# Projection of q, k, v in chunks of 512 columns instead of 384, with attention steps due at the ends of unbroken slots

## What is computed

```
hn   = rms_norm(x)                                  # 1024 x 1024
proj = hn @ w_in + b_in
q, k, v of 3 groups x 4 heads x 128 channels        # 12 units of 3 x 128 columns
q, k = rope(rms_norm(q)), rope(rms_norm(k))
out, lse = windowed attention of each group          # dilation 1, 4, 16
att  = softmax over the groups' lse, weighted sum of the outs
y_att = att * silu(z_att);  y_rnn = RG-LRU branch
x = x + (gate0 * (y_rnn @ w_o_rnn) + gate1 * (y_att @ w_o_att)) @ w_out
x = x + sigmoid(rms_norm(x) @ w_ple_gate + b) * (p @ w_ple)
```

## Time and profile before

| | us |
|---|---|
| median of 3 runs | 1463.46 |
| lowest and highest | 1462.47, 1465.11 |
| span of the profiled execution | 1463.9 |

### The profile page before, as it was taken

The page is one execution under the profiler, slowest core; times in us unless marked ns, Lnnn a source line. Parts: engine busy times, 40 slices in busy tenths (PEclk is TensorE's granted clock), DMA queues, the critical chain, the costliest instruction groups (busy, mean ns, idle before and its releaser), DMA issues.

```text
span 1463.9 us, 20230 instructions
## 1 busy us (share of the span) xinstructions
PE 1444.7 (99%) x6830; PEld 1282.4 (88%) x6830; DVE 833.2 (57%) x1698; ACT 455.9 (31%) x1162; POOL 507.7 (35%) x496
## 2 busy tenths in 40 slices
PE   8899999999999999999999999999999999999998
PEld 6688888999999999999999998888888888888887
DVE  5999998847764555654555666117822346325323
ACT  6345454533332332332322336520110001223100
POOL 6755544333321320330320433336543333243120
PEclk9999999999999999999999999999999999999999
DMA  6222312241211111110110113246628843321111
GB/s 230 80 79 80 106 61 96 86 128 50 64 42 37 49 44 49 49 53 26 49 52 32 58 58 116 87 144 244 222 79 327 305 151 108 122 72 37 51 51 43
DMA packets 67354, 139.76 MB, mean 95 GB/s; under 512 B 8672, under 2 KB 22976, under 8 KB 67264
## 3 DMA queue, kind: packets, MB, share of 16 engines
q10 hardware_dynamic: 29968, 75.89, 14.3%
q1 hardware_dynamic: 37296, 62.69, 13.6%
HBM read 109.04 MB, written 29.51 MB: 95 GB/s over the span
## 4 chain that ended last, share of the span: by engine, by line
PE 96%; DVE 2%; issue 0%; ACT 0%; DMA 0%; SPq 0%; DVEq 0%; ACTq 0%
PE bank L1068 30%; PE bank L1073 29%; PE bank L1072 29%; PE bank L1206 2%; PE bank L1186 2%; PE bank L1175 1%; PE bank L1195 1%; DVE xc L804 1%; PE bank L1293 0%; DMA x_nat<-in_x 0%; PE bank L1104 0%; DVE qkn L888 0%; DVE xc_lo L814 0%; DVE qks L902 0%; DVE qkr L901 0%
## 5 line engine op out<-in xcount | busy, mean ns | idle before, releaser
L398 POOL TENSOR_TENSOR w_lo<-raw,w_hi 128x512 fp32r<-128x512 f32 (+1 forms) x245 | 319.7, 1305 | 890.6 <-PE bank L1073 816.4
L1068 PE MATMUL bank<-w_hi,hn_hi 128*128 128x384 f32 x768 | 301.1, 392 | 0.0
L1073 PE MATMUL bank<-w_hi,hn_lo 128*128 128x384 f32 x768 | 290.7, 378 | 0.0
L1072 PE MATMUL bank<-w_lo,hn_hi 128*128 128x384 f32 x768 | 290.2, 378 | 0.0
L1068 PE MATMUL bank<-hn_hi,w_hi 128*128 128x512 f32 x640 | 251.6, 393 | 1.2 <-DVE hn_lo L749 1.2
L1073 PE MATMUL bank<-hn_hi,w_lo 128*128 128x512 f32 x640 | 249.7, 390 | 0.0
L1072 PE MATMUL bank<-hn_lo,w_hi 128*128 128x512 f32 x640 | 249.6, 390 | 0.0
L1072 PEld LDWEIGHTS bank<-w_lo,hn_hi 128*128 128x128 f32 x768 | 219.3, 286 | 0.0
L1073 PEld LDWEIGHTS bank<-w_hi,hn_lo 128*128 128x128 f32 x768 | 219.3, 286 | 0.0
L1068 PEld LDWEIGHTS bank<-w_hi,hn_hi 128*128 128x128 f32 x768 | 217.8, 284 | 0.1
L402 POOL TENSOR_SCALAR w_hi<-raw 128x512 fp32r<-128x512 f32 (+1 forms) x245 | 195.0, 796 | 9.1 <-DMA raw<-in_w_rnn_s 9.1
(11 more groups left out here) (176 smaller groups left out, 2097.7 us busy)
## 6 DMA issues: line engine op xcount, KB each, us to landing
raw<-in_w_tail_s SPq DMA_DIRECT2D x104, 256.0 KB, 2.6
raw<-in_w_qkv_s SPq DMA_DIRECT2D x96, 192.0 KB, 2.3
g_in<-gate_dram ACTq DMA_DIRECT2D x48, 256.0 KB, 3.0
raw<-in_w_rnn_s SPq DMA_DIRECT2D x45, 256.0 KB, 2.6
gate_dram<-g_out ACTq DMA_DIRECT2D x32, 256.0 KB, 2.0
o_dram<-o_buf ACTq DMA_DIRECT2D x12, 512.0 KB, 2.6
o_in<-o_dram ACTq DMA_DIRECT2D x12, 512.0 KB, 4.1
wt_in<-mw_dram ACTq DMA_DIRECT2D x12, 512.0 KB, 4.7
```

What stands on the lines that cost most here:

```text
L398: nc.gpsimd.tensor_tensor(w_lo[:, p % RING, 0:width], raw[:, p % RAW, 0:width], w_hi[:, p % RING, 0:width].bitcast(F32), ALU.subtract).the ...
L1068: ins = T.matmul(out, lhs[0], rhs[0], start=first, stop=False)
L1072: T.matmul(out, lhs[0], rhs[1], start=False, stop=False)
L1073: return T.matmul(out, lhs[1], rhs[0], start=False, stop=last)
```

## The change

- The 4608 columns of q, k, v are cut in 9 chunks of 512 (three to a group) instead of 12 units of 384: 72 slots of 24 matmuls with 512 columns. A chunk holds 4 parts of 128 columns, which belong to two heads; `part_of` and `parts_in` translate. Each weight piece is loaded by two DMAs from the unchanged array.
- The attention steps are no longer bound to slots. There are 101 steps (96 tiles and the last lag); step A stands behind the slot in which 90 + 6A blocks of contraction are done (`STEPS_AT`), so behind a slot come one or two steps, and they run on into the gate slots. The lags between parts are now counted in steps: 0 for the rotation, 1, 3, 4, 5. All three engines follow one list, `MAIN_ORDER`: slot, then its steps. DVE's work of a slot is `take_qkv`, ACT's the squares.
- In the gate slots ACT serves the gate first and then the steps. Two gates more stand before the first z, so two fewer after the last.
- qkv has three chunk buffers; to make room the ring has 12 pieces while q, k, v, gates and z run, outputs are written out in halves, and the rotation tables are held for one group at a time and loaded in halves.
- SP's and POOL's loops are written out instead of looped.

```diff
-LAG_T, LAG_QK, LAG_ET, LAG_PV = 9, 11, 12, 13
+LAG_T, LAG_QK, LAG_ET, LAG_PV = 1, 3, 4, 5
+STEPS = TILES + LAG_PV
+FIRST_STEP, STEP_BLOCKS = 90, 6
+STEPS_AT = [[A for A in range(STEPS) if -(-(FIRST_STEP + STEP_BLOCKS * A) // KD) == slot + 1]
+            for slot in range(SLOTS_Q + len(Z_MAIN))]
+
+
+def main_order():
+
+    order = []
+    for slot in range(SLOTS_Q + len(Z_MAIN)):
+        order.append(("slot", slot))
+        order += [("step", A) for A in STEPS_AT[slot]]
+    return order
...
+def ring_slot(p):
+
+    if p < FIRST_QKV:
+        return p % RING
+    if p < FIRST_O:
+        return (p - FIRST_QKV) % RING_Q
+    return (p - FIRST_O) % RING
...
-Z_MAIN = [(kind, t, h) for kind, t in [("gate", t) for t in range(10)]
-          + [("z", 0), ("gate", 10), ("z", 1), ("gate", 11), ("z", 2), ("gate", 12), ("z", 3)]
-          + [("gate", t) for t in range(13, 16)] for h in range(2)]
...
+Z_MAIN = [(kind, t, h) for kind, t in [("gate", t) for t in range(11)]
+          + [("z", 0), ("gate", 11), ("z", 1), ("gate", 12), ("z", 2), ("gate", 13), ("z", 3)]
+          + [("gate", t) for t in range(14, 16)] for h in range(2)]
...
+            for p in range(RAW, PIECES):
+                sp.wait_ge(w_ready, p + 1 - RAW)
...
+                    for u, col, width, dst in chunk_sources(c):
+                        sp.dma_start(raw[:, p % RAW, dst:dst + width], a["w_qkv_s"][u * KD + k, :, col:col + width]
+                                     ).then_inc(raw_in[p % RAW], 16)
...
+            for what, G in MAIN_ORDER:
+                if what == "step":
+                    attention(G)
+                    continue
+                if G < SLOTS_Q:
+                    if G >= 3:
+                        take_qkv(G)
+                    continue
...
-            for G in range(SLOTS_A):
-                u, s = divmod(G, NT)
-                grp = u // HEADS
+            for G in range(SLOTS_Q):
+                c, s = divmod(G, NT)
                 n = N_A + G
                 bank_free(n)
-                hi, lo = positions(grp, s, hn_hi), positions(grp, s, hn_lo)
+                hi, lo = positions(c // 3, s, hn_hi), positions(c // 3, s, hn_lo)
                 for k in range(KD):
-                    p = FIRST_QKV + KD * u + k
+                    p = FIRST_QKV + KD * c + k
                     need(p)
-                    ins = passes(bank[n % 4][:, 0:QKV], (hi(k), lo(k)),
-                                 (w_hi[:, p % RING, 0:QKV], w_lo[:, p % RING, 0:QKV]), k == 0, k == KD - 1)
+                    ins = passes(bank[n % 4][:], (hi(k), lo(k)), part(p), k == 0, k == KD - 1)
...
-                attention(G)
-
+                for A in STEPS_AT[G]:
+                    attention(A)
```

More of the change, by code:

```diff
@@ L59 @@
 RING = 16
+RING_Q = 12
 FIRST_QKV = PIECES_RNN
@@ L107, in has_prev, with part_of, parts_in, chunk_sources @@
     return (g == 0 and tile > 0) or (g == 1 and tile % 2 == 1)
+def part_of(u, x):
+    g, h = divmod(u, HEADS)
+    c, b = divmod(3 * h + x, CHUNK)
+    return 3 * g + c, b
+def parts_in(c):
+    g, r = divmod(c, 3)
+    return [(HEADS * g + (CHUNK * r + b) // 3, (CHUNK * r + b) % 3, b) for b in range(CHUNK)]
+def chunk_sources(c):
+    g, r = divmod(c, 3)
+    u, col = HEADS * g + CHUNK * r // 3, CHUNK * r % 3 * HD
+    width = 3 * HD - col
+    return (u, col, width, 0), (u + 1, 0, HALF - width, width)
+def raw_count(p):
+    loads = [2 if FIRST_QKV <= o < FIRST_TAIL else 1 for o in range(p % RAW, p + 1, RAW)]
+    return 16 * sum(loads)
+def units_after(c):
+    g, r = divmod(c, 3)
+    return [HEADS * g + h for h in ((0,), (1, 2), (3,))[r]]
+def std_count(u):
+    return 3 * (u // HEADS) + (0, 1, 1, 2)[u % HEADS] + 1
 def group_rows(stat, w, g, hd):
-    first = (w * SLOTS_A + (g * HEADS + hd) * NT) * P
+    first = (w * TILES + (g * HEADS + hd) * NT) * P
     classes = CLASSES[g]
@@ L373, in _ @@
                 sp.dma_start(dst[:], a[src]).then_inc(chan_in, 16)
[L374 to L387, removed]
+            for c in range(2):
+                sp.dma_start(bias_qkv[:, c], chunk_bias(c)).then_inc(bq_in[c], 16)
+            for p in range(RAW, PIECES):
+                sp.wait_ge(w_ready, p + 1 - RAW)
+                if p < FIRST_QKV:
+                    load(p % RAW, a["w_rnn_s"][p])
+                elif p < FIRST_TAIL:
+                    c, k = divmod(p - FIRST_QKV, KD)
+                    for u, col, width, dst in chunk_sources(c):
+                        sp.dma_start(raw[:, p % RAW, dst:dst + width], a["w_qkv_s"][u * KD + k, :, col:col + width]
+                                     ).then_inc(raw_in[p % RAW], 16)
+                else:
+                    load(p % RAW, a["w_tail_s"][p - FIRST_TAIL])
         @block.gpsimd
@@ L435, in _ @@
+            for p in range(PIECES):
+                pool.wait_ge(raw_in[p % RAW], raw_count(p))
+                if slot_before(p) is not None:
+                    pool.wait_ge(w_used, slot_before(p) + 1)
+                if p == FIRST_O:
+                    pool.wait_ge(pv_done, TILES)
+                if p >= 1:
+                    lo_part(p - 1)
+                hi_part(p)
+            lo_part(PIECES - 1)
         @block.scalar
@@ L543, in _, with attention @@
+            def attention(A):
+                for half in range(2):
+                    g, r = divmod(A - 1 + (NT // 2) * (1 - half), HEADS * NT)
+                    if r == 0 and 1 <= g < GROUPS:
+                        act.wait_ge(qkr_done, A - 1)
+                        load_cossin(g, half)
+                g = A - LAG_T
+                if 0 <= g < TILES:
                     act.wait_ge(tq_done, g + 1)
```

370 lines of the change are left out of this document (185 added, 185 removed).

## The result

The changed kernel takes 1483.2 us against 1464.2 of the kernel before, ratio 1.0127, 95% interval 1.0113 to 1.0142: slower by 19 us, where 8 were forecast. The profiled execution has a span of 1482.5 us, 18.6 more than the 1463.9 before.

A forecast was written before the change was run, and what follows sets the result against it. The prediction took TensorE (PE), with 96% of the chain, as the bound. Fewer blocks (-96.4), a credit (-1.9) and waits (+93.1) gave -5.2; with +13.3 for the clock, 1463.9 became 1472 us, range 1462 to 1486.

The forecast's parts named there:

- Fewer blocks: Projections: 72 blocks instead of 96 save 96.4 us, if strided loads keep their pace with 512 columns streaming.
- Waits: Second steps of pairs and steps behind bursts add 93.1 us; 1.9 us that PE lost before is credited.
- Plain pairs: Two steps behind an ordinary projection slot end at t+4.25 in group 2, 4.5 in group 1, 4.72 in group 0.
- Gate pairs: Four pairs between gate slots: the second step ends at t+5.3 against 1.38, 15.6 us in all.
- Single steps behind a burst: Five chunk ends: rotation ends at t+7.4, the late step costs 1.1 us each, 5.5 us in all.
- full burst pairs: Slots 23, 47, 71, fully in weight splitting: 4.7 us more each, 14.1; half ones, slots 32 and 56: 4.8 together.
- Clock: Idle PE falls to the 1.2 GHz level 10 times, costing 13.3 us.
- E: Rival: the clock falls after nearly every pair, 25 times, 33 us instead of 13, total 1492 us; chance 0.15.
- the ring of 12: 12 weight pieces instead of 16, costed at nothing; if the cover goes, up to 1 us at 8 chunk ends.
- B: Rival: the clock holds except in the three 6 us waits, total 1463 us; chance 0.22.
- D: Rival: weight load and moving stream share a path, so blocks grow to 7.0 us, +61, total 1533 us; chance 0.07.
- C: Rival: second steps wait only for the rotated tile, 15 us less, total 1457 us, 1448 with few falls; chance 0.14.

The follow-up runs named there:

- experiment 9: Changed kernel with TensorE computing only 384 of each projection slot's 512 columns and the weight ring back at its old address: 1438.9 us.
- experiments 7: Changed kernel with the weight ring back at its old address, unsplit pieces and constants again at the buffer's end: 1472.8 us.
- experiment 8: Changed kernel with 64 bytes more in front of the weight ring, so it and all behind start on multiples of 128 bytes: 1473.2 us.
- Experiment 1: Changed kernel with unread filler matmuls on PE between the two steps of each pair: 1466.0 us.
- experiment 12: Changed kernel with steps inside slots and ring at its old address (1384.9 us), plus input-row loads issued four gate steps later: 1380.5 us.
- experiment 10: Changed kernel with GpSimd splitting only the first 64 of 512 columns of each q, k, v weight piece: 1471.8 us.

## Why the prediction was right and wrong

The sign, the mechanism (the wait of the second step and the clock behind it) and the range held, but the size did not: +19 us, not +8. What failed are the terms put at nothing: the growth of the blocks beside 512 columns (7.2 us, nearly all of it strided ones), the moved buffers (4.6 us in the blocks) and everything outside the stage (8.6 us in the profiled executions). The waits, taken 11 us too high, hid as much again, so that the forecast came within 11 us of the result is in part luck. By its own terms:

- **Fewer blocks, -96.4: wrong, -84.6.** "I take no growth" failed. A strided load does cost more beside 512 columns than beside 384, by 0.09 and 0.15 us a block (experiment 9), far from the bound of 1.28 (24 x 0.053) but not nothing: against the values taken from the rows 24 x (0.02 + 0.11 + 0.17) = 7.2 us of the miss. The other 24 x (0.12 + 0.07) = 4.6 are the ring's 64 bytes (experiments 7, 8), for which the prediction has no term at all: the new addresses in the diff were read as a move only. The two independent ports of the Trainium skill, page "TensorE: Matmul & The Clock Gate", section "Step-by-step: what each phase is for", weighed in the prediction, hold nearly: by that rule the 0.09 and 0.15 would be nothing, by the shared path 1.28.
- **Waits, +93.1 - 1.9: too high by 11.** Plain pairs came as computed, mostly 4.25 in group 2 and 4.5 to 4.8 elsewhere, three of them 5.1 to 5.5. Gate pairs took 4.06 us, not 5.3 (-5.0): the prediction let ACT load the sigmoid's table after the pair's start, as at 881.97. ACT does it before, while it waits for the slot's end, so the copy is done at t+1.7 instead of t+2.8 and PE waits 0.94 us for it and 1.08 for the exponential.

```profile
882.34 1.28 ACT L686 ACT_TABLE_LOAD   x1
...
884.91 0.38 PE L1253 MATMUL bank<-ident,qkr 128*128 128x128 f32 x2
...
886.78 0.41 PE L1253 MATMUL bank<-ident,qkr 128*128 128x128 f32 x2 [0.94 <-ACT qkT L606]
...
888.50 0.33 PE L1273 MATMUL bank<-ident,probs 128*128 128x128 f32 x1 [1.08 <-ACT probs L616]
```

  Single steps behind a burst cost 0.75 us in all, not 5.5 (-4.8): the rotation, priced from 876.08 at t+7.4, was done at t+6.1 (slot 23) to t+6.9 (slot 15), so that it just fits in the 6.95 us until the transpose behind slot 16. For the same reason full burst pairs took 8.92, 7.97 and 7.45, 3.2 less than computed; the half ones took 7.94 and 7.62, 2 more. One row from one burst had priced eight places.
- **Clock, +13.3: right in sum.** 13 falls at 1.1 us, 14.6, against 10 at 1.33; they came elsewhere than thought, one between gates where three were expected and seven behind plain pairs of the stage. All 5 burst pairs and 8 of the 20 others lose the clock; which of these 8 is not told by their length (behind 4.05, 4.25 and 4.49 us it fell, behind others of the same length it held), and that stays open. E's 25 falls did not come. Experiment 1 takes the term away alone.
- **Outside the stage, 0: wrong, +8.6.** 2.5 in the recurrent part, which is within the scatter of single executions there: with the changed kernel's addresses the stage started at 275.3 us in the mean of seven, with the ring aligned at 273.5 in the mean of five, so some 2 us may be the alignment, and that stays open. 6.1 behind the statistics: 2.7 the new wait for g_in (experiment 12), and the other 3.4 fit the alignment, though they were not taken apart (the stretch falls by 8.1 with the ring at its old address, the wait still in it, by 4.4 with 64 bytes more, where that wait is 4.1 us and a low clock follows it, and the kernel before had the ring alone aligned). The prediction costed the ring of 12 at nothing by looking at chunk ends of the q, k, v stage only; the store that it lacks was felt, as far as the counts of experiment 12 tell, some 300 us after the stage, in a stretch where DMA is full.

The misses: 11.8 - 10.8 + 1.3 + 8.6 - 0.3 = 10.6, which is the 18.6 measured in the profile less the 8.1 forecast. Two errors of 11 us cancelled inside the stage, and what was left is the 8.6 us outside it. With the 64 bytes put right the changed kernel takes 1473 us (experiment 8). Of the rivals, B and E are ruled out by the 13 falls, D by blocks of 5.9 and 6.1 us instead of 7.0, C by the plain pairs at full length.

## What to carry to other kernels

Price a new order of work by the second request, not the first: two steps in a row wait for everything between them, and idle TensorE can then cost a second time at the lower clock; spread over the slot, the same steps took 98 us instead of 173. When a diff moves buffers, compare each start address with the old one at 64 or 128 bytes: that alone was 10 us of 1480. And look at a smaller prefetch store in the stage where DMA is full too, not only where the store shrinks.

## What the hardware showed that was not expected

- With the ring and all behind it 64 bytes off a multiple of 128, an undisturbed block of 24 matmuls took 5.69 us instead of 5.57 in group 0 and 5.92 instead of 5.85 in group 1, and the whole kernel 10 us more; group 2 (6.09, 6.08) and the gate blocks (5.59, 5.57) hardly changed. Nothing in the profile names it; only the pace shows it. Of what PE reads in these blocks only the weights had moved, and in the gate blocks, where they are the stationary side, they cost next to nothing: so it is likely the moving side that has to be aligned, but no run moved one buffer alone.
- While GpSimd splits, some of DVE's operations on two tiles in SBUF take three times as long or more, and those with an operand from a bank don't:

```profile
441.18 1.35 POOL L464 TENSOR_TENSOR ring<-raw,ring 128x512 fp32r<-128x512 f32 x1 [0.17 <-POOL ring L468]
441.44 1.37 DVE L967 TENSOR_TENSOR qkr<-qkn,cossin 128x256 f32<-128x256 f32 x1
...
445.96 0.42 DVE L991 COPY probsT<-bank 128x256 f32<-128x256 f32 x1
...
447.62 0.42 DVE L967 TENSOR_TENSOR qkr<-qkn,cossin 128x256 f32<-128x256 f32 x1
```
  With the splits cut short (440.34 in experiment 10) L967 takes 0.42 us, and so does the one at 447.62: not every operation is hit. The long ones of this burst start while POOL runs its TENSOR_TENSOR and end 0.1 to 0.3 us behind it (442.81 here, against 442.53). By the Trainium skill, page "GPSIMD Engine Reference", section "1. Specifications", GpSimd shares its way to SBUF with VectorE and disturbs its instructions with two SBUF inputs: this trace agrees, 1.37 against 0.42.
